# Seven block products instead of eight for the last 1024 columns of the values and of the keys and values

## What is computed

```
def chunk_gmlp(x, w_in, ...):
    uv = jax.nn.gelu(x @ w_in)              # (544, 1024) @ (1024, 4096)
    u, v = uv[..., :D_A], uv[..., D_A:]     # v: 2048 columns
    v = layernorm(v, ln_g, ln_b)
    ...
def kv_project(h, pos, kv_norm, kv_w, ...):
    kv = (rmsnorm(h, kv_norm) @ kv_w)       # (544, 1024) @ (1024, 1536)
    ...
```

## Time and profile before

| | us |
|---|---|
| median of 3 runs | 1541.11 |
| lowest and highest | 1540.86, 1542.75 |
| the profiled execution | 1539.93 |
| its span | 1538.1 |
| TensorE busy | 1508.9 (98%) |
| VectorE busy | 1051.4 (68%) |
| ScalarE busy | 640.4 (42%) |

### The profile page before, as it was taken

One profiled execution on the slowest core, in us unless ns is written; L12 is line 12 of the kernel. 1 busy time (PEld: TensorE's weight loads), 2 busy tenths in 40 slices (PEclk: granted clock), 3 DMA queues, 4 the chain that ended last, 5 costly groups with the idle time before them and its releaser, 6 DMA issues.

```text
span 1538.1 us, 28834 instructions
## 1 busy us (share of the span) xinstructions
PE 1508.9 (98%) x11746; PEld 1380.4 (90%) x11746; DVE 1051.4 (68%) x1567; ACT 640.4 (42%) x1067; POOL 94.5 (6%) x155
## 2 busy tenths in 40 slices
PE   9999999999999999999999999998999999999998
PEld 6779999999999999998777756776799999999998
DVE  5339753368877869756266777877668969778952
ACT  6335311233333324334344667776543334333422
POOL 0000000000000000000000125553000000000000
PEclk9999999999999999999999999999999999999999
DMA  5438222322231323232315613104542232323232
GB/s 171 159 105 300 63 83 83 100 82 83 69 121 58 124 91 95 76 110 82 110 61 159 175 57 110 56 1 140 153 121 83 69 96 83 110 69 124 81 101 69
DMA packets 127816, 157.09 MB, mean 102 GB/s; under 512 B 11930, under 2 KB 102386, under 8 KB 127282
## 3 DMA queue, kind: packets, MB, share of 16 engines
q1 hardware_dynamic: 127346, 155.29, 31.7%
q10 hardware_dynamic: 352, 0.15, 0.0%
HBM read 149.58 MB, written 14.16 MB: 106 GB/s over the span
## 4 chain that ended last, share of the span: by engine, by line
PE 91%; DVE 5%; ACT 2%; issue 1%; DMA 0%; POOL 0%; SPq 0%; DVEq 0%; ACTq 0%
PE PS L754 40%; PE PS L1067 21%; PE PS L786 13%; PE PS L1383 2%; PE PS L1398 2%; PE PS L1300 2%; PE PS L1355 1%; PE PS L796 1%; PE PS L1263 1%; PE PS L1004 1%; PE PS L1366 1%; DMA xtok<-in_x_prompt 0%; PE PS L1518 0%; PE PS L1495 0%; PE PS L1461 0%
## 5 line engine op out<-in xcount | busy, mean ns | idle before, releaser
L2161 DVE TENSOR_TENSOR wl<-raw,wh 128x2048 fp32r<-128x2048 f32 (+2 forms) x89 | 167.9, 1887 | 128.4 <-ACT wh L1653 85.1
L1633 ACT ACTIVATE wh<-raw 128x2048 fp32r<-128x2048 f32 (+2 forms) x73 | 110.4, 1513 | 227.7 <-PE PS L754 140.5
L2212 DVE TENSOR_TENSOR hT<-PS,hT 128x544 f32<-128x544 f32 (+1 forms) x104 | 75.1, 722 | 130.4 <-PE PS L754 130.0
L1067 PE MATMUL PS<-opL,whA 128*128 128x272 f32 x512 | 148.7, 290 | 0.0
L1067 PE MATMUL PS<-opH,whA 128*128 128x272 f32 x512 | 147.8, 289 | 0.4 <-DVE wlB L2477 0.4
L1067 PE MATMUL PS<-opH,wlA 128*128 128x272 f32 x512 | 147.8, 289 | 0.0
L754 PE MATMUL PS<-act0h,wh 128*128 128x272 f32 x640 | 133.5, 290 | 0.4 <-DVE sg L2369 0.4
L754 PE MATMUL PS<-act0l,wh 128*128 128x272 f32 x640 | 132.3, 288 | 0.0
L754 PE MATMUL PS<-act0h,wl 128*128 128x272 f32 x640 | 132.3, 288 | 0.0
L1067 PE MATMUL PS<-opL,whB 128*128 128x272 f32 x384 | 111.5, 290 | 0.0
L1067 PE MATMUL PS<-opH,wlB 128*128 128x272 f32 x384 | 110.8, 289 | 0.0
(11 more groups left out here) (416 smaller groups left out, 3688.6 us busy)
## 6 DMA issues: line engine op xcount, KB each, us to landing
raw<-in_ffn_w_gate SPq DMA_DIRECT2D x44, 512.0 KB
raw<-in_ffn_w_up SPq DMA_DIRECT2D x44, 512.0 KB
raw<-in_a_w_in SPq DMA_DIRECT2D x32, 512.0 KB, 4.7
raw<-in_ffn_w_down SPq DMA_DIRECT2D x64, 256.0 KB
raw<-in_a_w_out SPq DMA_DIRECT2D x16, 512.0 KB
crows<-in_cache_kv_cmp SPq DMA_DIRECT2D x32, 256.0 KB, 2.9
cache<-in_state_kv_win SPq DMA_DIRECT2D x8, 1024.0 KB, 7.5
out_kv_win_sample<-in_state_kv_win SPq DMA_DIRECT2D x8, 1016.0 KB
```

Of the source, the lines that this page charges most:

```text
L1067: mm = pe.matmul(PS[:, bank, 0:HALF], w, X[:, x, k, :], start=(k == 0 and not last and X is opH), stop=(k == 3 and last))
L1633: act.activation(wh[:, rs, 0:kn, :], raw[:, rs, 0:kn, :], ACT.Copy).then_inc(w_hi, 1)
L2161: dve.tensor_tensor(wl[:, rs, 0:kn, :], raw[:, rs, 0:kn, :], wh[:, rs, 0:kn, :].bitcast(F32), ALU.subtract).then_inc(w_ready, 1)
L2212: dve.tensor_tensor(h, psum_u(s, mt), h, ALU.add).then_inc(free[s], 1)
```

## The change

Value groups 2 and 3 (columns 1024 to 2047) and key groups 1 and 2 (columns 512 to 1535) become one unit each. A unit multiplies the 512 prompt tokens by 1024 columns as a 2x2 block product: token halves by halves of the 1024 model columns (four k-tiles each), and weight halves of 512 columns. It does so with seven products of 256 tokens x 512 x 512 (24 matmuls each, `unit_b`) instead of eight. For that:

- `unit_sums_made` (VectorE) makes four sums and differences of token blocks from `hT` and the gains, 24 operations of 128x256, into the part of `vt` or `kvtok` that the unit fills later; `unit_sums_high` (ScalarE) and `unit_sums_low` (VectorE) split them. They stand in `segment_wide` behind the split of item 0, in the first of the two value groups that stay and in the one key group that stays.
- the weight blocks are loaded into the two slots and, one of them, into a buffer `second`; VectorE forms their sums T1 to T4 in place, and each of the seven operands is split (the fifth in two halves, so eight items).
- the products are joined (U2, U4, C12, C22, U3, C11, C21) by seven additions of VectorE out of PSUM into `vt` or `kvtok`; ScalarE then applies gelu and scale in place.
- the item behind a unit (`u.item + 8`, in slot 0) is loaded once item 7 of the unit is split, and its split stands behind the join C11.
- `wsraw` is loaded later, since `second` lies where it goes.
- two of the statistics on the sample tokens are made twice.

The core of the diff:

```diff
+        def unit_blocks(u, w, c):
+
+            sp.wait_ge(w_ready, u.item + 1)
+            sp.wait_ge(f_mm, u.few_mm - 1)
+            block([wide(raw, 0)[:, k:k + 1, :] for k in range(4)], w, 0, c, loaded[0], 64)
+            block([x[:, :, :] for x in u.r2], w, 0, c + 2 * CW, s_first, 32)
+            sp.wait_ge(w_ready, u.item + 2)
+            sp.wait_ge(f_mm, u.few_mm)
+            block([wide(raw, 1)[:, 2 * j:2 * j + 2, :] for j in range(2)], w, 4, c + 2 * CW, loaded[1], 32)
+
+        def unit_last_block(u, w, c):
+
+            sp.wait_ge(w_ready, u.item + 3 + 3)
+            sp.wait_ge(f_mm, u.few_mm + 3)
+            block([wide(raw, 1)[:, 2 * j:2 * j + 2, :] for j in range(2)], w, 4, c, loaded[1], 96)
 
...
             sp.dma_start(bsrow[g0:g0 + GA, :], a_b_spatial[0]).then_inc(s_bias, 16)
         sp.dma_start(ptab[:, :], page_table.rearrange("(o b) g -> o (b g)", o=1)).then_inc(s_ptab, 16)
 
+        unit_last_block(unit_v, a_w_in[0], DA + 1024)
+        sp.wait_ge(w_ready, unit_v.item + 5 + 3)
+        sp.dma_start(wsraw[:, :, :], a_w_spatial[0].rearrange("g t s -> t g s")).then_inc(s_misc, 16)
+        sp.wait_ge(w_ready, unit_v.item + 7 + 3)
         for m in range(4):
...
+            pe.wait_ge(s_first, u.second + 64)
+            pe.wait_ge(wide_few, u.few_n)
+            partials(WIDE_GATHER, 0, lambda j: u.r2[j // 2][:, j % 2, :], True)
+            pe.wait_ge(loaded[1], 32 * u.item + 64)
+            partials(WIDE_GATHER, 1, lambda j: wide(raw, 1)[:, j, :], False)
+            pe.wait_ge(wide_free, u.stored - (u.item == unit_v.item) * QT)
+            product(0, block(0, 0), a)
+            pe.wait_ge(wide_free, u.stored)
+            product(1, made(0), b)
+            product(2, made(1), c)
+            pe.wait_ge(wide_free, u.stored + 1)
+            product(3, made(3), a, after=lambda: gather(0))
+            pe.wait_ge(k_sq, u.joins + U4)
+            product(4, made(2), b, ks=range(2))
+            product(5, made(2), b, ks=range(2, 4), slot=2)
+            pe.wait_ge(loaded[1], 32 * u.item + 256)
+            partials(WIDE_FEW, 1, lambda j: wide(raw, 1)[:, j, :], False)
+            product(6, block(1, 0), c)
+            pe.wait_ge(k_sq, u.joins + U3)
+            product(7, block(1, 1), b, after=lambda: gather(1))
+
...
+        def unit_sums_high(u):
+
+            act.wait_ge(k_sq, u.joins + MADE)
+            for j in range(4):
+                ins = act.activation(u.S[j][0][:, :, :], u.x_sum[j], ACT.Copy)
+            ins.then_inc(k_sd, 1)
...
+            act.wait_ge(k_sq, u.joins + T1)
+            unit_split(u, 1, r0, 0)
+            few_high(WIDE_GATHER, u.few_mm + 3)
+            act.wait_ge(k_sq, u.joins + T2)
+            unit_split(u, 2, r0, 1)
+            act.activation(u.dst[:, 0:2, c1:c1 + 512], PS[:, a:a + 2, :], ACT.Copy).then_inc(wide_free, 1)
+            act.wait_ge(loaded[1], 32 * u.item + 64)
+            unit_split(u, 3, r1, 2)
+            act.wait_ge(k_sq, u.joins + T3)
+            act.wait_ge(wide_mm, u.tiles + 3)
+            act.activation(wide(wh, 0)[:, 0:2, :], u.r2[0][:, :, :], ACT.Copy).then_inc(w_hi, 1)
+            act.wait_ge(wide_mm, u.tiles + 4)
+            act.activation(wide(wh, 1)[:, 0:2, :], u.r2[1][:, :, :], ACT.Copy).then_inc(w_hi, 1)
+            few_stored(0, c2)
+            stored(C12, 0, c2, 2)
+            act.wait_ge(loaded[1], 32 * u.item + 256)
+            unit_split(u, 6, r1, 5)
+            few_high(WIDE_FEW, u.few_mm + 4)
+            act.wait_ge(k_sq, u.joins + T4)
+            unit_split(u, 7, r0, 6)
+            stored(C22, 1, c2, 2)
+            after(0)
+            stored(C11, 0, c1, 2)
+            few_stored(1, c1)
+            stored(C21, 1, c1, 1)
+            after(1)
+
+        def segment_wide(at, pairs, dst, func, part, f0, i0, p0, u=None):
 
             for p in range(pairs):
                 wide_partials(part, f0 + 2 * p + 2)
-                wide_split(0, at[0] + 2 * p + 2, wide_done, 2 * (p0 + p) + 1)
+                if u is not None and p == pairs - 1:
+                    act.wait_ge(loaded[0], 32 * u.item + 256)
+                    act.wait_ge(wide_done, 2 * (p0 + p) + 1)
+                    act.activation(wide(wh, 0), wide(raw, 0), ACT.Copy).then_inc(w_hi, 1)
+                else:
+                    wide_split(0, at[0] + 2 * p + 2, wide_done, 2 * (p0 + p) + 1)
+                if u is not None and p == 0:
...
                 act.wait_ge(wide_done, 2 * (p0 + p) + 2)
                 act.activation(dst[:, QT, c], PS[:, WIDE_GATHER, :], func,
                                scale=stats[:, C_RS + QT:C_RS + TT]).then_inc(wide_few, 1)
-                wide_split(1, at[0] + 2 * p + 3, wide_mm, i0 + QT * p + QT)
+                if u is None or p < pairs - 1:
+                    wide_split(1, at[0] + 2 * p + 3, wide_mm, i0 + QT * p + QT)
+            if u is not None:
...
+        def unit_sums_made(u):
+
+            x = lambda i, j, k: hT[:, 4 * j + k, 2 * P * i:2 * P * i + 2 * P]
+            g = lambda j, k: gains[:, u.gain + 4 * j + k:u.gain + 4 * j + k + 1]
+            s1, s2, s3, s4 = u.x_sum
+
+            def fused(out, i, j, k, other, op):
+                link.put(dve.scalar_tensor_tensor(out=out[:, k, :], in0=x(i, j, k), scalar=g(j, k), in1=other, op0=ALU.mult, op1=op))
+
+            for k0 in range(0, 4, 2):
+                for k in range(k0, k0 + 2):
+                    for n, (i, j) in enumerate(((1, 1), (0, 0))):
+                        link.put(dve.tensor_scalar(u.x_part[:, 2 * (k - k0) + n, :], x(i, j, k), g(j, k), None, ALU.mult))
+                link.settle()
+                for k in range(k0, k0 + 2):
+                    fused(s1, 1, 0, k, u.x_part[:, 2 * (k - k0), :], ALU.add)
+                    fused(s3, 1, 0, k, u.x_part[:, 2 * (k - k0) + 1, :], ALU.subtract)
+                link.settle()
+                for k in range(k0, k0 + 2):
+                    fused(s2, 0, 0, k, s1[:, k, :], ALU.subtract)
+                link.settle()
+                for k in range(k0, k0 + 2):
+                    fused(s4, 0, 1, k, s2[:, k, :], ALU.add)
+                link.settle()
+            dve.memset(small[:, 1, 3:4], 0.0).then_inc(k_sq, 1)
+
...
+                                  part[0][:, :, :].rearrange("p s n -> p (s n)").bitcast(F32), ALU.subtract).then_inc(f_lo, 2)
+
+            dve.wait_ge(f_mm, u.few_mm + 1)
+            dve.wait_ge(s_first, u.second + 64)
+            dve.wait_ge(w_ready, u.item + 3)
+            for j in range(2):
+                half = dve.tensor_tensor(r0[:, 2 * j:2 * j + 2, :], u.r2[j][:, :, :], r0[:, 2 * j:2 * j + 2, :], ALU.subtract)
+            half.then_inc(k_sq, 1)
+            low(1, r0)
+            dve.wait_ge(w_ready, u.item + 4)
+            dve.wait_ge(loaded[1], 32 * u.item + 64)
+            joined(r0, r0, r1, ALU.subtract, T2)
+            dve.wait_ge(f_mm, u.few_mm + 3)
+            for j in range(2):
+                half = dve.tensor_tensor(u.r2[j][:, :, :], u.r2[j][:, :, :], r1[:, 2 * j:2 * j + 2, :], ALU.subtract)
+            half.then_inc(k_sq, 1)
+            few_low(WIDE_GATHER, u.few_mm + 2)
+            low(2, r0)
+            low(3, r1)
+            dve.wait_ge(wide_mm, u.tiles + 3)
+            dve.wait_ge(wide_free, u.stored + 1)
+            joined(m2, c, m1, ALU.add, U2)
+            joined(u4, b, m2, ALU.add, U4)
+            low(4, u.r2[0][:, :, :], 2)
+            dve.wait_ge(wide_mm, u.tiles + 4)
+            joined(m3, a, u4, ALU.add, C12)
+            low(5, u.r2[1][:, :, :], 2)
+            dve.wait_ge(loaded[1], 32 * u.item + 256)
+            joined(r0, r0, r1, ALU.add, T4)
+            low(6, r1)
+            dve.wait_ge(wide_mm, u.tiles + 6)
+            joined(u4, b, u4, ALU.add, C22)
+            joined(m2, b, m2, ALU.add, U3)
+            few_low(WIDE_FEW, u.few_mm + 4)
+            low(7, r0)
+            stat(1, (2,), (0, 1), 1)
+            dve.wait_ge(wide_mm, u.tiles + 7)
+            joined(m1, c, m1, ALU.add, C11)
+            split(0, u.item + 8)
+            stat(1, (2,), (2, 3), 3)
+            stat(0, (), (0, 1), 5)
+            dve.wait_ge(wide_mm, u.tiles + 8)
+            joined(m2, b, m2, ALU.add, C21)
+            stat(0, (1,), (2, 3), 7)
+            split(1, u.item + 9)
+
...
+        def segment_wide(at, pairs, part, f0, evac=None, u=None, stat=None):
 
             for p in range(pairs):
                 wide_partials(part, f0 + 2 * p + 2)
                 split(0, at[0] + 2 * p + 2)
+                if u is not None and p == 0:
+                    unit_sums_made(u)
+                    unit_sums_low(u)
                 if evac is not None:
                     evac(p)
-                split(1, at[0] + 2 * p + 3)
+                if u is None or p < pairs - 1:
+                    split(1, at[0] + 2 * p + 3)
+            if u is not None:
+                unit_wide(u, part, stat)
 
```

162 lines of the change are left out of this document (139 added, 23 removed).

## The result

The changed kernel takes 1572.17 us (median of 4 runs, 1571.02 to 1574.09), the kernel before 1540.99 in the same session: a ratio of 1.0201, 95% interval 1.0183 to 1.0219: slower, though the interval leaves open whether by 2% or by a little less. The forecast was 1570.5. The profiled execution is 32.6 us longer than that of before, where the sum gave 29.4.

What follows compares the result with a forecast made beforehand. TensorE, busy 98% of the span, was taken to bound the kernel. Values +14.0 and keys +15.3, together +29.4 us on the profiled 1539.93, gave 1569.3; with 1.2 for the median, 1570.5 us, range 1560 to 1578.

Steps and rivals of the forecast that it cites:

- What is removed: TensorE: 24 matmuls fewer in the values and 24 in the keys, 48 x 0.234 = 11.2 us saved.
- The sums' price: VectorE ahead of each unit: making the four sums of activations takes 9.5 us.
- The bound for the one-input operations: VectorE's eight one-input operations per unit: 2.3 us taken, bounds 1.9 (the 128-wide price) and 3.4 us.
- rival of cheap two-input operations: VectorE's sums take only 5.2 us, each stall 4.3 us shorter: 1562 us; chance 9%.
- The place, values, +10.1: Value group 1: added work delays the second split to 61.0 where TensorE wants it at 50.9, costing 10.1 us.
- clock rival: Granted clock falls to 1.2 GHz behind TensorE's new waits: up to +8 us, 1578; 15% for over 3 us.
- The place, keys, +14.8: Key unit's start: ScalarE stores group 0 only behind the sums' high parts; TensorE stops from 733.45 to 748.2, +14.8 us.
- Inside the units, +3.0 and +3.4: Within the units, products wait for operands to be formed and split: +3.0 us in the values, +3.4 in the keys.
- The ends, +2.8 and +2.7: Unit ends: next load waits for the last operand's low part in slot 0; +2.8 us values, +2.7 keys.
- VectorE's chain in the values, +3.4: Behind the value unit: VectorE reaches the aggregation at 132.8 instead of 117.46, with nothing to absorb it, +3.4 us.
- The cover holds: Rival: in both stages the added sums lie in the engines' idle time; faster, 1530 to 1536 us; chance 4%.

Runs made afterwards that it cites:

- e10: e8 with the keys' eight low parts of act1 moved inside the unit and all the sums' low parts before its first split: 1535.02 us, 0.9965 of before.
- e1: Changed kernel without the 24 operations making the sums, in both units; high and low parts made from slices of hT instead: 1553.1 us.
- e3: Changed kernel, keys only: sums before the few tokens' low part, their high parts behind group 0's stores, low parts behind the first subtraction: 1559.78 us.
- e4: Changed kernel plus 72 unread matmuls filling TensorE's waits: 60 in the keys' long wait, 12 at the key unit's end: 1577.59 us.
- e5: Changed kernel with T4 written to two spare tiles instead of weight slot 0 in both units, so the next load needn't wait: 1564.74 us.
- e9: Changed kernel plus only 12 unread matmuls, in the wait at the key unit's end: 1572.41 us.
- e2: Changed kernel, values only: the sums moved behind the second split of group 1, their high and low parts later too: 1566.5 us.
- e7: Changed kernel with the sums placed as in e6 and the unit ends as in e5: 1538.45 us, 0.9994 of before.
- e8: e7 with VectorE reordered: T3 before the first low part; in the keys, token squares between the sums' halves, low parts earlier: 1538.03 us, 0.9986 of before.
- e6: Changed kernel with the sums and their high and low parts placed elsewhere in both units, some group 1 statistics later, nothing left out: 1548.49 us.

## Why the prediction was right, point by point

- **What is removed.** 48 matmuls at 0.234 us. The page of the profile has 48 fewer, and e10, whose clock is full throughout, has 11.1 us less of busy time.
- **The sums' price.** Forecast 9.5 us; measured 37.31 to 46.8, 9.5. The bound for the one-input operations held too: 0.28 us each, my value was 0.27 apart. The rival of cheap two-input operations falls by this row, and e1 shows that the price is paid about one to one.
- **The place, values, +10.1.** The second split ended at 61.0, as laid out. The first wait is 7.4 us as forecast. The second, of 2.7 us from 58.3, isn't there: the lower clock (0.50 until 58.6) stretched the matmuls in between by as much, so that it cost nothing, as the clock rival's "covered" part said. The total of this term came out without that part of its path. In e3, e4, e5 and e9, where the lower clock ended at 56 to 57 already, a wait of 0.5 to 0.9 us for this split does stand there.
- **The place, keys, +14.8.** The wait is 15.3, and a wait of 0.36 us for the split stands ahead of it, so the place costs 15.6, not 14.8. ScalarE's high part starts 1.0 us later against TensorE than in the earlier trace rows (742.85 - 14.3 = 728.6, where it was 727.59), since the load lands later; the prediction had taken it as landing at the same time. The load is made of four transfers now, with more behind them; whether that delays it isn't shown.
- **Inside the units, +3.0 and +3.4.** From the start of the unit's first matmul to that of its last there would be 43.7 us without waits (the 49.55 of the earlier trace rows less 25 x 0.234). In the values it takes 46.7 (72.86 to 119.52), 3.0 more: waits of 0.45, 1.69 and 0.56 at the places named, and their ends. In the keys it takes 47.2 beside the long wait (747.15 to 809.66, less 15.26), 3.6 more, of other make: 2.4 are slow matmuls at its start, and only 0.9 waits, since the operands were ready when the slow products ended.
- **The ends, +2.8 and +2.7.** Measured 3.3 and 2.9, and undone by e5.
- **VectorE's chain in the values, +3.4.** TensorE's shift is 11.2 us at the first product of the mix (123.26, before 112.11) and 14.4 at 174.26, so 3.2 came behind the unit, where the aggregation stood at 133.19. On TensorE's side they look like 1.6 of waiting (at 147.27, for VectorE) and some 1.5 of slow matmuls (clock 0.50 from 123.4 to 126.8). But the chain on VectorE sets the sum: in e2, where the clock stays full behind the same wait, TensorE waits for VectorE for the whole of it:

```profile
131.23 0.69 PE L1106 MATMUL PS<-wsT,early 4*32 4x32 f32 x16 [1.35 <-DVE wsT L2720]
139.80 0.47 PE L1120 MATMUL PS<-bsr,pick 128*128 128x512 f32 x1 [1.68 <-DVE bsr L2736]
```

No run takes this term away by itself.

- **The term that was mis-sized: the keys, 15.3 forecast, 18.3 measured.** The 3.0 are 0.8 of the place (the load), 0.2 inside, 0.2 to 0.3 at the end, and 1.7 of slow partials in the query group, the one term that the sum did not have at all (e9, e4 and e5 take it away). The clock rival had its mechanism right and its place wrong: it priced the long wait of the keys at up to 7.5, where the slow products only took the place of waits for VectorE, and left out the short wait of 2.9 us at the unit's end, behind which everything is due at once. The Trainium skill ("TensorE: Matmul & The Clock Gate", section "Loop structure matters more than you think") says that matmuls behind a long wait run cold. The traces agree for the long waits, of 5.2 us and more; behind waits near 3 us the runs show both (below).
- **How close the number is.** On profiled executions the sum was 3.2 us short (32.6 for 29.4; its own terms, 14.0 and 15.3, add up to 29.3). On the medians it is 1.7 us short, since the profiled execution of before lies 1.2 us under its median and that of after 0.4 over its own. That part of the closeness is luck.
- **The side.** "The cover holds" failed as an account of this kernel: idle time of 65 to 79% helped nothing, for the reason given, the order. As an account of what the change could be it is nearer: e10 reaches 1535, inside the 1530 to 1536 that the rival gave; e7 and e8, at 1538, stay above it.

## What to carry to other kernels

A share of idle time says only that a place for added work exists, not that the work is in it: find for each added block the next instruction on the same engine for which someone waits, and its slack. Here the same operations cost 31 us or saved 5, by their place and by the buffer of one operand. When one blocker is moved, read the next in the list before the run (e2 and e3 fell 4.5 and 2.3 us short of what was expected for not doing so), and once an engine has no idle time between two due dates, take work out of the stretch instead of ordering it anew.

## What the runs showed of the hardware

- The lower clock is not a factor of two for these matmuls: at a granted clock of 0.50 they start 0.43 us apart, at 1.00 0.234, a factor of 1.83; sixteen partials of the few tokens go from 1.92 to 3.58 us.
- Whether a wait brings it varies. Behind each of the 14 waits of 5.2 to 15.3 us in these traces the granted clock was 0.50. Of the ten between 2.6 and 3.4 us seven brought it: behind 2.84 us the sixteen partials of the query group ran slow in e2 and at full clock in e3 (1.93 us), behind 3.34 us the first products of the mix ran slow in after and behind 3.32 at full clock in e2, and behind 2.61 (e8) the first eight matmuls ran at full clock and the granted clock fell 1.2 us after they began. Behind most waits of 1.2 to 1.8 us it stayed full, but it fell behind 1.61 (e9, e6) and 1.68 (e2). So the length of a short wait does not tell; what else decides is not shown.
- Two loads of 1 MB issued back to back (the mix's first items) took the first one 4.7 to 5.0 us to land in three kernels (after, e2, e6) and 6.8 to 7.1 in four (e1, e3, e4, e9), with the same issue times against each other. That is 2 us on the profiled execution, as much as some of the edits. With one trace of each kernel it isn't shown whether it belongs to the kernel or to the execution.
- Adding 72 matmuls that fill waits (e4) went with an attention stage 300 us later that took 4.4 us longer, and adding 12 (e9) with 1.3 longer. The 1.3 are a fall of the clock, and so are 1.3 of the 4.4; the two waits behind the rest (0.74 and 1.83 us) stay unexplained.
